# The expert loop of a pooling and mixture-of-experts block: three small GpSimd copies per step, and the places of the lower half of h and of the copy of Y

## The reference

```python
h = rms_norm(x, norm_mix)
x = x + pool_mixer(h, pool_w, pool_scale)        # trailing means of 2/4/8/16 tokens, then 4 products 256x256
h = rms_norm(x, norm_ffn)                        # "normed"
# router: best of 4 groups, then the best 2 of its 8 experts; gate weights from both softmaxes
for each expert e of 32:                         # each token goes to 2 experts
    g, up = split(h[rows_of_e] @ w_gu[e])        # w_gu[e]: 1024 x 1024 f32
    y = (silu(g) * up) @ w_down[e]               # w_down[e]: 512 x 1024 f32
    total[rows_of_e] += y * gate
out = rms_norm(total, norm_final)
```

## Time and profile before

| what | value |
|---|---|
| time of the profiled execution | 665.68 us |
| its span, first to last instruction | 663.7 us |
| median of the three timed runs | 666.05 us |
| granted TensorE clock, mean | 0.986 |
| TensorE busy | 634.7 us, 96% |
| VectorE busy | 602.8 us, 91% |
| ScalarE busy | 531.1 us, 80% |
| GpSimd busy | 298.6 us, 45% |
| moved by DMA | 242.83 MB, mean 366 GB/s |
| copies `dst_now`, `src_now`, `gate_now` | 29 each, 49.1, 47.9 and 35.6 us |

### The profile page before, as it was taken

The page is one execution under the profiler, slowest core; times in us unless marked ns, Lnnn a source line. Parts: engine busy times, 40 slices in busy tenths (PEclk is TensorE's granted clock), DMA queues, the critical chain, the costliest instruction groups (busy, mean ns, idle before and its releaser), DMA issues.

```text
span 663.7 us, 9755 instructions
## 1 busy us (share of the span) xinstructions
PE 634.7 (96%) x3524; PEld 538.4 (81%) x3524; DVE 602.8 (91%) x497; ACT 531.1 (80%) x454; POOL 298.6 (45%) x211
## 2 busy tenths in 40 slices
PE   7899989999999999999999999999999999987993
PEld 5899978887888888888888888888888887876872
DVE  6887789989989989989989989989989979979897
ACT  6996626679879879879879879879879869857794
POOL 5000010055444654654754654654654875781401
PEclk9999989999999999999999999999999999997997
DMA  8997859998999999999999999999999999999875
GB/s 302 418 420 267 273 188 392 381 366 279 341 361 393 387 413 403 386 410 405 380 411 397 374 392 402 372 385 394 376 393 384 387 388 389 401 400 398 318 300 208
DMA packets 44148, 242.83 MB, mean 366 GB/s; under 512 B 8695, under 2 KB 9855, under 8 KB 19522
## 3 DMA queue, kind: packets, MB, share of 16 engines
q1 hardware_dynamic: 34322, 220.39, 83.6%
q0 software_dynamic: 9776, 21.79, 12.0%
HBM read 228.24 MB, written 27.26 MB: 385 GB/s over the span
## 4 chain that ended last, share of the span: by engine, by line
PE 78%; DVE 13%; ACT 3%; issue 3%; DMA 2%; POOL 0%; SPq 0%; ACTq 0%; DVEq 0%; POOLq 0%
PE psum L1720 56%; DVE w_lo L1206 8%; PE psum L1732 8%; PE psum L1772 4%; PE psum L1648 3%; PE psum L1783 2%; PE psum L1666 2%; PE psum L1634 2%; DMA pw_in<-in_pool_w 1%; PE psum L1657 1%; DVE raw L1544 1%; PE psum L1674 1%; ACT end_junk L819 1%; DMA out<-raw 1%; ACT w_hi L887 1%
## 5 line engine op out<-in xcount | busy, mean ns | idle before, releaser
L1206 DVE TENSOR_TENSOR w_lo<-raw,w_hi 128x2048 fp32r<-128x2048 f32 x113 | 255.1, 2284 | 12.0 <-ACT w_hi L887 7.7
L887 ACT ACTIVATE w_hi<-raw 128x2048 fp32r<-128x2048 f32 x113 | 213.1, 1914 | 12.7 <-PE psum L1720 12.7
L1206 DVE TENSOR_TENSOR w_lo<-raw,w_lo 128x2048 fp32r<-128x2048 f32 x79 | 178.4, 2283 | 0.0
L739 POOL DMA_INDIRECT total<-ysb,dst_now x29 | 90.5, 3122 | 146.0 <-ACT ysb L983 146.0
L1720 PE MATMUL psum<-w_lo,x_hi 128*128 128x512 f32 x528 | 152.4, 392 | 0.0
L887 ACT ACTIVATE w_lo<-raw 128x2048 fp32r<-128x2048 f32 x79 | 149.0, 1914 | 2.6 <-PE psum L1720 2.6
L1720 PEld LDWEIGHTS psum<-w_lo,x_hi 128*128 128x128 f32 x528 | 98.4, 188 | 20.1
L1720 PE MATMUL psum<-w_lo,h_hi 128*128 128x512 f32 x376 | 108.3, 395 | 0.5 <-DVE h_lo L1476 0.5
L1720 PEld LDWEIGHTS psum<-w_lo,h_hi 128*128 128x128 f32 x376 | 70.4, 190 | 15.3 <-DVE h_lo L1476 0.9
L1720 PE MATMUL psum<-w_hi,x_hi 128*128 128x512 f32 x240 | 75.9, 398 | 0.0
L702 POOL DMA_INDIRECT xg<-normed,src_now x29 | 65.7, 2266 | 22.3 <-POOL src_now L710 22.3
(11 more groups left out here) (206 smaller groups left out, 955.9 us busy)
## 6 DMA issues: line engine op xcount, KB each, us to landing
raw<-in_expert_w_gu SPq DMA_DIRECT2D x128, 1024.0 KB, 11.0
raw<-in_expert_w_down SPq DMA_DIRECT2D x64, 1024.0 KB, 11.4
res<-in_x SPq DMA_DIRECT2D x8, 512.0 KB, 9.4
normed<-nx POOLq DMA_DIRECT2D x8, 512.0 KB, 7.8
total<-res SPq DMA_DIRECT2D x8, 512.0 KB, 8.7
raw<-total SPq DMA_DIRECT2D x8, 512.0 KB, 9.7
out<-raw SPq DMA_DIRECT2D x8, 512.0 KB, 3.1
pw_in<-in_pool_w SPq DMA_DIRECT2D x1, 1024.0 KB, 7.4
```

What stands on the lines that cost most here:

```text
L739: pool.indirect_dma_start(out=total[:, :], out_offset=bass.IndirectOffsetOnAxis(ap=dst_now[0:slots].bitcast(u32), axis=0), in_=ysb[0:slots ...
L887: nc.scalar.activation(hi_at(s0, j), raw[q][:], ACT.Copy).then_inc(hi_done, 1)
L1206: V.tensor_tensor(w_lo[q][:], raw[q][:], hi_at(s0, j).bitcast(f32), ALU.subtract)\
```

## The change

GpSimd no longer copies indices and gates in the main steps: the indirect DMAs take their indices from `src_all` itself, and ScalarE takes the gates from `gate_all`. Experts 3 and 0, whose table columns are rewritten in the meantime, keep their copies: `src_now` in step 0, `gate_now` and `dst_now` in `first_scatter`. ScalarE's wait for the gates is gone but for the first; in its place the second waits once for `pos_made`. In steps 4 to 30 ScalarE copies Y before it makes `h_hi`. VectorE makes `h_lo` behind one pair more. The loop for overflowing experts, which doesn't run with these inputs, is adapted.

```diff
-            def gather(s, g, copies, slots=P, rows=None):
-                rows = sources(s) if rows is None else rows
+            def gather(s, g, copies, rows):
                 nc.gpsimd.tensor_copy(src_now[:, g:g + 1], rows).then_inc(idx_now, 1)
                 pool.wait_ge(idx_now, copies)
-                gather_rows(g, src_now[:, g:g + 1], last_row(s, 1), slots)
+                gather_rows(g, src_now[:, g:g + 1], last_row(s, 1))
...
+            def first_scatter():
+                pool.wait_ge(gates_made, 1)
+                put(column(expert(0)), 2)
+                pool.wait_ge(res_stored, 16 * TILES)
+                pool.wait_ge(y_copied, 1)
+                scatter_rows(dst_now[:], TOKENS - 1)
+
+            def scatter(s):
+                pool.wait_ge(y_stored, s * 16)
+                pool.wait_ge(y_copied, s + 1)
+                scatter_rows(src_all[:, column(s)], TOKENS - 1, H if is_small(s) else P)
...
             def step(s, s0, turn):
-                if s0 < E - XG:
-                    if s0 == 1:
-                        scatter(0, 2, 0)
-                        pool.wait_ge(pos_made, 1)
+                if s == 1:
+                    first_scatter()
+                    pool.wait_ge(pos_made, 1)
+                if s < E - XG:
                     pool.wait_ge(x_turned, s + 1)
-                    gather(s + XG, s0 % XG, 3 if s0 == 1 else s * 2 if s0 else 1, H if is_small(s0 + XG) else P)
-                if 1 < s0 <= E - LATE:
-                    scatter(s - 1, s * 2 + 1 if s0 < E - XG else E - XG + s, s - 1,
-                            slots=H if is_small(s0 - 1) else P)
+                    if s == 0:
+                        gather(XG, 0, 1, src_all[:, column(expert(XG))])
+                    else:
+                        gather_rows(s % XG, src_all[:, column(s + XG)], TOKENS - 1, H if is_small(s + XG) else P)
+                if 1 < s <= E - LATE:
+                    scatter(s - 1)
...
-            def copy_y(puts, dn_end, stored, y=Y):
+            def copy_y(gates, dn_end, stored, y=Y):
                 act.wait_ge(pair_used, dn_end)
-                act.wait_ge(gate_put, puts)
                 if stored is not None:
                     act.wait_ge(y_stored, stored * 16)
-                nc.scalar.activation(ysb[:], y, ACT.Identity, scale=gate_now[:]).then_inc(y_copied, 1)
+                nc.scalar.activation(ysb[:], y, ACT.Identity, scale=gates).then_inc(y_copied, 1)
...
                 else:
+                    if s < E - 1:
+                        copy_y(gate_all[:, s - 2:s - 1], start(s), s - 2)
                     split_h_block(s - 1, start(s))
-                if s < E - 1:
-                    copy_y(s - 1, start(s), s - 2)
...
-                up_to(low_next, low_pair, s, n + 2)
+                up_to(low_next, low_pair, s, n + 3)
```

More of the change, by code:

```diff
@@ L692, in column @@
                 return slice(s, s + 1) if isinstance(s, int) else bass.ds(s, 1)
[L694 to L698, removed]
             def gather_rows(g, rows, most, slots=P):
@@ L735, in scatter, with scatter_rows, put @@
+            def scatter_rows(rows, most, slots=P):
+                pool.indirect_dma_start(
+                    out=total[:, :], out_offset=bass.IndirectOffsetOnAxis(ap=rows[0:slots].bitcast(u32), axis=0),
+                    in_=ysb[0:slots, :], in_offset=None, bounds_check=most, oob_is_err=False,
+                    compute_op=ALU.add).then_inc(y_stored, 16)
+            def put(col, copies):
+                nc.gpsimd.tensor_copy(gate_now[:], gate_all[:, col]).then_inc(gate_put, 1)
                 nc.gpsimd.tensor_copy(dst_now[:], src_all[:, col]).then_inc(idx_now, 1)
@@ L746, in _, with further_scatter @@
+            def scatter(s):
+                pool.wait_ge(y_stored, s * 16)
+                pool.wait_ge(y_copied, s + 1)
+                scatter_rows(src_all[:, column(s)], TOKENS - 1, H if is_small(s) else P)
+            def further_scatter(s, copies):
+                pool.wait_ge(y_stored, s * 16)
+                put(column(s), copies)
+                pool.wait_ge(y_copied, s - 1)
+                scatter_rows(dst_now[:], last_row(s, 2))
             pool.wait_ge(tables_made, 1)
@@ L807, in _ @@
                     pool.wait_ge(x_turned, v + E)
-                    gather(v + E, 0, v * 2 + (2 * E - XG - 2), rows=src_all[:, column(v + E)])
-                    scatter(v + E, v * 2 + (2 * E - XG - 1), v + E, further=True)
+                    gather(v + E, 0, v * 2 + 3, src_all[:, column(v + E)])
+                    further_scatter(v + E, v * 2 + 4)
         @block.scalar
@@ L974, in split_h_block, with gates_of_y @@
                     .then_inc(h_hi_done, 1)
-            def copy_y(puts, dn_end, stored, y=Y):
+            def copy_y(gates, dn_end, stored, y=Y):
                 act.wait_ge(pair_used, dn_end)
-                act.wait_ge(gate_put, puts)
                 if stored is not None:
                     act.wait_ge(y_stored, stored * 16)
-                nc.scalar.activation(ysb[:], y, ACT.Identity, scale=gate_now[:]).then_inc(y_copied, 1)
+                nc.scalar.activation(ysb[:], y, ACT.Identity, scale=gates).then_inc(y_copied, 1)
+            def gates_of_y(s):
+                if s == 0:
+                    act.wait_ge(gate_put, 1)
+                if s == 1:
+                    act.wait_ge(pos_made, 1)
             def early_step(s):
@@ L1001, in early_step @@
                     if s >= 2 and j == h_split_at(s):
-                        copy_y(s - 1, pair(s - 1, PER_STEP - 1) + 1, None if s == 2 else s - 2)
+                        gates_of_y(s - 2)
+                        copy_y(gate_now[:] if s == 2 else gate_all[:, s - 2:s - 1], start(s), None if s == 2 else s - 2)
                     if s == 0 and j == GU_PAIRS - 1:
@@ L1044, in step @@
                     act.wait_ge(pair_used, start(s))
-                    act.wait_ge(pos_made, 1)
                     act.wait_ge(y_stored, 16 * (E - LATE))
@@ L1094, in _ @@
                         over_pair(j)
-                    copy_y(v + (E - 2), first + PER_STEP, v + E, y=OVER_Y)
+                    act.wait_ge(gate_put, v + 2)
+                    copy_y(gate_now[:], first + PER_STEP, v + E, y=OVER_Y)
                 for i in range(TILES):
```

## The result

The changed kernel is slower: a median of 676.5 us in four runs (673.93 to 678.75), beside 665.9 us of the kernel before on the same chip (664.38 to 666.57). The ratio is 1.0164, 95% interval 1.0139 to 1.0188. The forecast was 661.7 us, with a range from 659.6 to 665.6; the result lies outside it, on the side that had a chance of 0.12. The profiled execution took 678.75 us, with a span of 676.8 us and a mean clock of 0.981.

A forecast was written before the change was run, and what follows sets the result against it. TensorE was taken as the bound, losing time to late `hid` and a lower clock. The last load caps the gain at 5.5 us, less 1.5 for gathers: 4.0 us, from 665.68 to 661.7 us; range 659.6 to 665.6.

The forecast's parts named there:

- What bounds the kernel: Late steps: TensorE loses 9.60 us to `hid` waits and lower clock, traced through ScalarE's copy of Y to held GpSimd instructions.
- The small copies alone are worth about 1 us and the landing takes the gates' place: Copies of Y at 539 and 592 us: then wait for scatter landings; about 1 us off 5.28; rival 664.7 us, chance 0.17.
- the trace disagrees on both: Against the skill's one-instruction port hold, with descriptor writing inferred free: a scatter was held 11.34 us, five `low_pair` long.
- ScalarE asks for it about 0.6 us sooner against VectorE's work: Scatter request after the reordering: about 0.6 us sooner, with `h_lo` still to come one or two pairs on.
- ScalarE's order costs nothing where s-1 is small: Small steps: `h_hi` waits 1.72 us for its transposes, so the 1.11 us copy of Y fits in.
- So the hold is at most 2 x 2.2 us: Scatter hold after the change: ends at `h_lo`, which has a PSUM input, one or two pairs of 2.2 us on.
- the landing about 4 + 8.3 us after the request: Scatter landing after the change: early enough that the copy of Y's waits of 4.75 and 5.28 us go.
- The copy of Y stops `h_hi`: Rival, steps 28 to 30: `h_hi` queues behind a waiting copy of Y; price 6.7 us, so 672.3 us; chance 0.12.
- In the middle this is worth 0: TensorE covers it: Middle of the run: removing some 130 us of GpSimd's small copies gains 0, TensorE being busy 20.00 us of 20.
- The cap by the last loads: Tail: at most 5.5 us before loads bound; late gathers push the last load 1.5 us, leaving 4.0 us.
- Elsewhere `h_hi` comes 1.1 us later. I cost this at 0: Steps where s-1 is not small: later `h_hi` priced at 0; without TensorE's cover up to 0.6 us a step.

The follow-up runs named there:

- A+B: Kernel after with the copy of Y put back behind `h_hi` (small copies gone, `h_lo` behind the fourth pair): 663.67 us, ratio 0.9957 to the kernel before.
- A alone: Kernel before with only the small copies taken out, both orders as before: 665.07 us, ratio 1.0000.
- the split of C: Kernel after with the copy of Y ahead of `h_hi` only where s-1 is small: 673.99 us, 1.0132; only where it is not: 665.38 us, 0.9991.
- C: The part that puts the copy of Y ahead of `h_hi`; as the only change to the kernel before: 689.12 us, ratio 1.0377.
- B alone: Kernel before with nothing but `h_lo` moved behind the fourth pair: 664.03 us, ratio 0.9984.
- A+C: Kernel after with `h_lo` put back behind the third pair (small copies gone, copy of Y first): 665.96 us, ratio 1.0014 to the kernel before.
- B+C: Kernel before with `h_lo` behind the fourth pair and the copy of Y ahead of `h_hi`, all small copies kept: 691.79 us, ratio 1.0389.

## Why the prediction was wrong, point by point

**What bounds the kernel: right.** TensorE is the bound, its losses are waits for `hid` and the clock behind them, and they come from GpSimd's held instructions by way of ScalarE's copy of Y. A+B removes the holds and brings TensorE back to 19.68 us of 20 at full clock from 600 to 620 us, against 16.05 at 0.83:

```profile
600.00:620.00 20.00, 19.68 (x94) 16.16 (x93) 18.18 (x11) 17.14 (x12) 3.35 (x1) 1.00 1.02 403
```

**The small copies alone are worth about 1 us and the landing takes the gates' place: right about the landing, the 1 us not to be seen.** In A alone the waits of 4.17 and 4.88 us are for the landing, and the second copy of Y starts at 591.87, where the landing was reckoned for 591.8; before it started at 592.69. The time, 1.0000 with 0.17% to either side, shows no gain and can't exclude one of 1 us. The prediction said that by the Trainium skill (SBUF — State Buffer, Who interferes with whom) the removed copies would be the whole gain and the place of `h_lo` worth nothing. No run bears that out. Taking the copies away left both holds as they were, and moving `h_lo` besides ended both. But "the trace disagrees on both" went too far. The scatter takes its indices from `src_all`, a table in SBUF, so its hold may be one of GpSimd's reads, which by the prediction's own sentence the port does block. No run separates reading indices from writing descriptors. What the rows do contradict is the length, one instruction at a time.

**"ScalarE asks for it about 0.6 us sooner against VectorE's work": the failed step, first half.** I counted `h_hi`'s own 0.6 us and left out the 1.72 us that it waits for its transposes in a small step, though the same paragraph names them. The copy used to stand behind this wait and now goes ahead of it. From the small step's `hid` to the scatter it is 2.37 us at the first hold of the kernel after and 4.69 us in A+B: 2.3 us sooner, and the wait and `h_hi` account for 2.2 of them. At the second hold it is 1.70 us, 3.0 us sooner; ScalarE was by then farther ahead of VectorE. "ScalarE's order costs nothing where s-1 is small" was the conclusion I drew. It costs ScalarE nothing there; what it does to the scatter is most of the loss, as the split of C shows (1.0132 against 0.9991).

**"So the hold is at most 2 x 2.2 us": the failed step, second half.** I took it that the next VectorE instruction with an input in PSUM lets GpSimd in. That had been seen with `hid`, behind which `x_lo` follows, also with a PSUM input; for `h_lo`, alone between pairs, I had shown no row. The trace before has one, of a copy and not of a scatter, in the fence below: the copy ends 0.06 us after `h_lo` begins. In the kernel after all eight held scatters passed `h_lo` and took 11.35 to 14.24 us, where the bound was 4.4. Doubling the instruction at this place ended seven of the eight holds at 4.6 us.

```profile
315.92 4.68 POOL L735 COPY dst_now<-src_all 128x1 int32<-128x1 int32 x1 [2.59 <-DMA total<-ysb,dst_now]
320.54 0.69 DVE L1476 TENSOR_TENSOR h_lo<-psum,h_hi 128x512 fp32r<-128x512 f32 x1
```

The two halves belong together. From the bound came "the landing about 4 + 8.3 us after the request", hence no wait for a landing, and the stop of `h_hi` had a chance of only 0.12. What the runs showed in its place are landings 20.80 us after the request (the second hold), eight waits of ScalarE for them, 48.5 us, and a loss of 1.64%.

**The rival "The copy of Y stops `h_hi`": the right mechanism, with the wrong place, count and chance.** Its deciding point was right. A release 4.8 us after the request was to be the limit. By the prediction's own reckoning, by which a scatter is released 0.5 us before its row ends (2.52 less a hold of 2.0), the one in the episode above was released 11.5 us after its start, 6.7 us too late, and ScalarE stood 6.71 us. That the two agree so well is in part luck: the copies of Y would have been 1.0 us farther apart than reckoned, and the landing took 1.0 us longer. The place was said to be steps 28 to 30, "where nothing is in hand"; it is every small step. The price was said to be 6.7 us once; it is about 11 us in eight pieces, some 1.3 us each: TensorE has work in hand that covers most of each delay of ScalarE, and what passes costs a wait (1.94 us in the episode, 3.70 the longest) and some clock. "In the middle this is worth 0: TensorE covers it" was true of the copies' own time. I let the same cover stand for stalls of 6 us in the middle, and never worked out how large a stall it takes.

**The cap by the last loads: right, with a smaller size.** In A+B the last load is issued at 617.7 and lands at 629.9, and ScalarE splits it at once:

```profile
630.03 1.92 ACT L884 ACTIVATE w_hi<-raw 128x2048 fp32r<-128x2048 f32 x1 [0.32 <-PE psum L1724]
```

This is 1.96 us before the 631.99 of the earlier trace rows; I had said 4.0. In that execution the loop began 1.7 us late behind the setup stage, which is most of the difference. The last load was issued 3.4 us later than before; 1.7 us of this is the late start, and the other 1.7 are near the 1.5 us that the prediction took for the gathers and the read of `total`. By the medians A+B gains 0.43% or 2.9 us (1.1 to 4.6). Without C in the change the forecast of 661.7 would have been some 2 us low, and the range would have held the result.

**The price of C in the other steps: right within some 2 us.** "Elsewhere `h_hi` comes 1.1 us later. I cost this at 0": the run with C only there is at 0.9991, A+B at 0.9957, intervals that overlap a little, so these 2 us are hardly more than the noise.

## What to carry to other kernels

When an instruction is moved, follow not only who waits for it but when it now asks a slow partner for something. Here a copy moved into an idle gap cost its own engine nothing and sent a DMA request 2.3 to 3.0 us earlier, to the start of a run of VectorE work instead of its end. An engine that waits for the landing of a DMA should have its longest hold priced, not its median, and a second buffer takes the wait away without ending the hold. "TensorE covers it" needs a size: here it covered ScalarE's pauses of 1.7 us in the small steps and not those of 6.7.

## What the runs showed of the hardware

- GpSimd's indirect DMA, and its copies of a single column, can be held for many VectorE instructions with both inputs in SBUF: up to 14.24 us for a scatter and 16.06 us for a copy of 128x1, where the shortest took 1.5 and 0.18 us. The Trainium skill (SBUF — State Buffer, Who interferes with whom) speaks of one instruction at a time; the measurement decides.
- In the kernel after a single VectorE instruction with a PSUM input (`h_lo`, a row of 0.68 us) ended none of the eight holds. Two in a row did, both where the kernel has them (`hid` and `x_lo`) and where one was added: the scatter ended some 1.5 us after the first of them began. Whether it is their number or the length of the stretch was not tried.
- The same lone `h_lo` can let GpSimd in. In B alone five held copies of one column ended 0.1 us after it began (7.05 us from 218.59, `h_lo` at 225.51). In A+C six scatters, asked for 1.4 us ahead of it, ended 1.5 us after it began (2.94 us from 220.82, `h_lo` at 222.25). In B+C such a copy passed it (13.89 us from 216.93, `h_lo` at 223.50) and ended when `hid` began.
- Why some requests are let in at the next change between instructions and others not stays open. In A+C one scatter at the same distance to VectorE's instructions was held 12.34 us, and those of the small steps before and after it were not. No run separates this.
